# A fifth slot of split weights around three layer boundaries

## What is computed

```python
x = layer_norm(ALPHA * x + h, ln_g[i], ln_b[i])       # h = (o * silu(gate)) @ w_o
x = x + (p[i] @ w_ple[i]) * jax.nn.sigmoid(x @ w_ple_gate[i])
# next block
h = _rmsnorm(x, pre_mix_g) * (1.0 + scale_a) + shift_a
proj = h @ w_in                                        # its first columns: the stage c_f
```

## Time and profile before

| | |
|---|---|
| median of three runs | 2229.97 us (2229.56 to 2232.17) |
| profiled execution, its time | 2231.24 us |
| its span, first to last instruction | 2229.4 us |
| PE busy | 2181.2 us (98%) |
| DVE busy | 1442.8 us (65%) |
| ACT busy | 1011.1 us (45%) |
| mean granted PE clock | 0.995 |

### The profile page before, as it was taken

How to read it: one execution, slowest core, us unless ns; L and a number is a source line. 1 busy time by engine, 2 the same in 40 slices (tenths; PEclk the granted TensorE clock), 3 DMA queues, 4 the chain that set the end, 5 groups by cost and what they waited for, 6 DMA issues and landing times.

```text
span 2229.4 us, 24586 instructions
## 1 busy us (share of the span) xinstructions
PE 2181.2 (98%) x10387; PEld 1811.5 (81%) x10387; DVE 1442.8 (65%) x1420; ACT 1011.1 (45%) x996; POOL 6.5 (0%) x17
## 2 busy tenths in 40 slices
PE   8999999999999999999999999989999999999998
PEld 8878888777888788777888988867888888888887
DVE  5778667775755777767966775487545544544656
ACT  5443563433436633434454566544434434443442
POOL 0000000000000000000000000000000000000000
PEclk9999999999999999999999999999999999999999
DMA  8867649475966466758853325365556656655753
GB/s 287 309 242 270 240 151 388 179 287 193 371 255 238 170 246 268 277 211 329 338 179 104 122 93 196 118 236 213 203 190 231 224 186 215 244 185 199 266 179 125
DMA packets 73310, 499.36 MB, mean 224 GB/s; under 512 B 8945, under 2 KB 9457, under 8 KB 16369
## 3 DMA queue, kind: packets, MB, share of 16 engines
q1 hardware_dynamic: 72784, 497.66, 61.5%
q10 hardware_dynamic: 416, 0.13, 0.0%
HBM read 493.52 MB, written 4.24 MB: 223 GB/s over the span
## 4 chain that ended last, share of the span: by engine, by line
PE 93%; DVE 5%; ACT 2%; issue 1%; DMA 0%; ACTq 0%; DVEq 0%; SPq 0%
PE products L2336 68%; PE products L2347 14%; PE aside L2653 1%; PE transposed L2772 1%; PE transposed L2410 1%; DVE w_low L1422 1%; ACT w_high L839 1%; PE transposed L2500 1%; PE aside L2500 1%; PE transposed L2468 1%; DVE x_low L1538 0%; PE products L2759 0%; PE aside L2759 0%; PE aside L2940 0%; PE transposed L2930 0%
## 5 line engine op out<-in xcount | busy, mean ns | idle before, releaser
L1422 DVE TENSOR_TENSOR w_low<-raw,w_high 128x2048 fp32r<-128x2048 f32 (+3 forms) x336 | 744.2, 2218 | 566.1 <-ACT w_high L839 565.0
L839 ACT ACTIVATE w_high<-raw 128x2048 fp32r<-128x2048 f32 (+3 forms) x336 | 622.4, 1855 | 821.2 <-PE products L2336 668.3
L2336 PE MATMUL products<-w_high,x_high 128*128 128x512 f32 (+2 forms) x1688 | 651.2, 386 | 12.3 <-DVE w_low L1422 9.7
L2336 PE MATMUL products<-w_high,x_low 128*128 128x512 f32 (+2 forms) x1688 | 644.0, 382 | 0.0
L2336 PE MATMUL products<-w_low,x_high 128*128 128x512 f32 (+2 forms) x1688 | 643.6, 381 | 0.0
L2336 PEld LDWEIGHTS products<-w_high,x_high 128*128 128x128 f32 x1688 | 318.2, 189 | 73.3 <-issue 14.2
L2336 PEld LDWEIGHTS products<-w_high,x_low 128*128 128x128 f32 x1688 | 318.2, 188 | 60.1
L2336 PEld LDWEIGHTS products<-w_low,x_high 128*128 128x128 f32 x1688 | 318.4, 189 | 59.4 <-issue 1.4
L1436 DVE SCALAR_TENSOR_TENSOR raw<-raw,cond_row 128x2048 f32<-128x2048 f32 x96 | 220.2, 2294 | 0.4 <-DMA raw<-in_w_mod 0.3
L2347 PE MATMUL products<-w_high,x_high 128*128 128x512 f32 (+1 forms) x472 | 192.7, 408 | 11.4 <-DVE w_low L1422 5.9
L2336 PE MATMUL products<-w_high,u_high 128*128 128x512 f32 x496 | 193.7, 391 | 0.0
(11 more groups left out here) (439 smaller groups left out, 1898.6 us busy)
## 6 DMA issues: line engine op xcount, KB each, us to landing
raw<-in_w_mlp SPq DMA_DIRECT2D x128, 1024.0 KB, 4.9
raw<-in_w_mod SPq DMA_DIRECT2D x96, 1024.0 KB, 5.2
raw<-in_w_ple SPq DMA_DIRECT2D x32, 1024.0 KB, 7.0
raw<-in_w_a_qkv SPq DMA_DIRECT2D x24, 1024.0 KB, 6.2
raw<-in_w_b_kvq SPq DMA_DIRECT2D x24, 1024.0 KB, 7.3
raw<-in_w_a_gate SPq DMA_DIRECT2D x16, 1024.0 KB, 5.7
raw<-in_w_a_out SPq DMA_DIRECT2D x16, 1024.0 KB, 7.1
raw<-in_w_b_gate SPq DMA_DIRECT2D x16, 1024.0 KB, 5.7
```

The source lines that it names most:

```text
L839: act.activation(split_tile(m, 0, st, u, j, 0, n), m.raw[:, RAW_SLOT[at], 0:n], ACT.Copy).then_inc(m.s_w_high, 1)
L1422: dve.tensor_tensor(lo, m.raw[:, RAW_SLOT[at], 0:n], hi.bitcast(F32), ALU.subtract).then_inc(m.s_raw_used, 1)
L2336: ins = pe.matmul(bank, x[:, x0 + kk, a], w, start=first and kk == 0 and n == 0, stop=last and kk == st.kq - 1 and n == 2)
```

## The change

Two more pieces of the arena become slots: `SPARE_SLOTS` 0 is the old extra slot, 1 serves `a_out` and `b_out` (from the fourth quarter on) and the first unit of `ple0` and `ple1`, 2 serves `c_f` from its second quarter to the end of its second unit. With it, quarter 1 of the next stage's first unit is split before row block 0's norm, on ACT and DVE, and `rows_in` is reordered on both. Transpose 3 moves from the last k-tile of half 2 to its second. Since slot 2 lies on the buffer of `h_spans`, that table is loaded after `c_f`'s last unit, into the place of slot 0.

```diff
+SPARE_SLOTS = ((18432, 20480), (13312, 15360), (8192, 6144))
+def slots_for(name, u, j):
+    out = name in ("a_out", "b_out") and (u, j) >= (0, 3)
+    spare = (out or name in ("ple0", "b_kvq", "ple1") or (name == "c_f" and u < 2),
+             out or (name in ("ple0", "ple1") and u == 0),
+             name == "c_f" and (0, 1) <= (u, j) < (2, 0))
+    return [k for k in range(RING)] + [RING + n for n, free in enumerate(spare) if free]
...
-TURNS_AHEAD = {0: (2, 2), 2: (3, 3), 3: (2, 4), 4: (2, 5), 5: (2, 6), 6: (2, 7)}
+TURNS_AHEAD = {0: (2, 2), 2: (1, 3), 3: (2, 4), 4: (2, 5), 5: (2, 6), 6: (2, 7)}
...
@@ sync_program @@
     def c_rows():
         sp.wait_ge(m.s_y_ready, 20)
+        sp.wait_ge(m.s_w_used, 4 * PLAN["ple1"].g0 + 8)
...
-    sp.wait_ge(m.s_ple_full, 8)
-    for dr in range(2):
-        bring(m.h_md_in[dr][:], ...)
     sp.wait_ge(m.s_x4_ready, 4)
...
+            if name == "c_f" and u == 3:
+                sp.wait_ge(m.s_w_used, 4 * (PLAN["c_f"].g0 + 2) + 4)
+                for dr in range(2):
+                    bring(m.h_md_in[dr][:], ...)
@@ pool_program @@
     pool.wait_ge(m.s_h_md_landed, 32)
-    pool.wait_ge(m.s_w_used, 4 * (PLAN["c_f"].g0 + 2) + 4)
@@ scalar_program @@
-        gemm(name_out, nothing, late=3)
+        gemm(name_out, nothing, late=2)
...
             if (layer, 2 * i + k) == (1, 3):
+                act.wait_ge(m.s_ple_full, 8)
+                high_unit("c_f", 0, [1])
                 act.wait_ge(m.s_first_rows, 3)
...
         std(0, 1)
-        high_unit(name, 0, [1])
+        high_unit(name, 0, [2])
         row_high(ROWS_THREE, [0, 1])
-        high_unit(name, 0, [2])
         if between:
             between()
         row_high(ROWS_THREE, [2])
@@ vector_program, rows_in @@
         whole(0)
         normalise(0, 1)
-        low_unit(following, 0, [1])
+        normalise(0, 2)
+        low_unit(following, 0, [2])
         row_low(ROWS_THREE, 0)
-        normalise(0, 2)
         row_low(ROWS_THREE, 1)
-        low_unit(following, 0, [2])
+        whole(1)
         row_low(ROWS_THREE, 2)
-        whole(1)
         normalise(1, 1)
         row_low(ROWS_THREE, 3)
         normalise(1, 2)
+        low_unit(following, 0, [3])
         row_low(ROWS_THREE, 4)
         normalise(0, 3)
         row_low(ROWS_THREE, 5)
-        low_unit(following, 0, [3])
         normalise(1, 3)
...
-        gemm(name_out, add, late=3)
+        gemm(name_out, add, late=2)
...
             if (layer, u) == (1, 3):
+                low_unit("c_f", 0, [1])
                 return
```

More of the change, by code:

```diff
@@ L131 @@
 RAW_SLOT, RAW_COUNT, RAW_BEFORE, RAW_LAST = raw_plan()
[L134 to L141, removed]
+SPARE_SLOTS = ((18432, 20480), (13312, 15360), (8192, 6144))
[5 more added lines that the diff above has]
+    return [k for k in range(RING)] + [RING + n for n, free in enumerate(spare) if free]
 def ring_plan():
-    slots, before, last = [], [], [-1] * (RING + 1)
+    slots, before, last = [], [], [-1] * (RING + len(SPARE_SLOTS))
     for st in PLAN.values():
@@ L150, in ring_plan @@
             for j in range(4):
-                places = range(RING + 1 if has_extra(st.name, u, j) else RING)
-                k = min(places, key=lambda i: last[i])
+                k = min(slots_for(st.name, u, j), key=lambda i: last[i])
                 slots.append(k)
@@ L183, in split_tile @@
     k = slot(st, u, j)
-    if k == EXTRA_SLOT:
-        return (m.hi_extra, m.lo_extra)[which][:, first:last]
+    if k >= RING:
+        return m.spare[k - RING][which][:, first:last]
     return (m.hi, m.lo)[which][:, k, first:last]
@@ L337, in memory @@
     m.hi, m.lo = sb("w_high", [P, RING, 2048], F32R), sb("w_low", [P, RING, 2048], F32R)
-    m.hi_extra, m.lo_extra = at("w_high_extra", 18432, [P, 2048], F32R), at("w_low_extra", 20480, [P, 2048], F32R)
+    m.spare = [[at(f"w_{part}_spare_{n}", word, [P, 2048], F32R) for part, word in zip(("high", "low"), words)] for n, words in enumerate(SPARE_SLOTS)]
     m.xh, m.xl = sb("x_high", [P, KT, T], F32R), sb("x_low", [P, KT, T], F32R)
@@ L439, in memory @@
     m.b_og = at("b_out_gated", 20736, [P, 2, RB, GROUP * HD])
-    m.h_md_in = [at(f"h_spans_in_{dr}", 6144 + 1152 * dr, [P, 9, P]) for dr in range(2)]
+    m.h_md_in = [at(f"h_spans_in_{dr}", 18432 + 1152 * dr, [P, 9, P]) for dr in range(2)]
     m.h_md = at("h_spans", 18432, [P, 2, 9, P], F32R)
@@ L750, in sync_program @@
     gemm("ple1", c_rows)
-    sp.wait_ge(m.s_ple_full, 8)
-    for dr in range(2):
-        bring(m.h_md_in[dr][:], d.spans[:, 9 * P * dr:9 * P * (dr + 1)].rearrange("p (b c) -> p b c", b=9), m.s_h_md_landed)
     sp.wait_ge(m.s_x4_ready, 4)
@@ L765, in unit_by_unit @@
                     bring(m.h_l0[:, dr, slot, :], rows(lb[slot], 1024), m.s_h_rows)
+            if name == "c_f" and u == 3:
+                sp.wait_ge(m.s_w_used, 4 * (PLAN["c_f"].g0 + 2) + 4)
+                for dr in range(2):
+                    bring(m.h_md_in[dr][:], d.spans[:, 9 * P * dr:9 * P * (dr + 1)].rearrange("p (b c) -> p b c", b=9), m.s_h_md_landed)
     for name in ("c_f", "c_hq", "c_hi", "c_mla", "c_hg", "uq", "ukv"):
```

## The result

| | median, us | runs | lowest to highest |
|---|---|---|---|
| before | 2230.05 | 15 | 2229.22 to 2232.17 |
| changed | 2233.95 | 15 | 2231.95 to 2236.82 |

The ratio is 1.0018, 95% interval 1.0010 to 1.0025: 3.9 us slower, between 2.2 and 5.6. The forecast was 2229.8 with a range up to 2232.9. The profiled execution of the changed kernel took 2232.58 us (span 2230.8), 1.4 less than its median; the profiled one of before took 1.2 more than its own.

A forecast was written before the change was run, and what follows sets the result against it. PE holds 93% of the chain, so only its waits and the clock could move, 11.5 us at most. -1.4 (`ple0`, `ple1`), -0.2 (`c_f`) and +1.4 (table) gave -0.2: 2229.8 us, range 2226.8 to 2232.9.

The forecast's parts named there:

- The waits of `ple0` and `ple1`: At these two boundaries PE's waits were to sum to 1.81 against 2.50 us, a gain of 0.7 each, -1.4.
- It just fits: At `ple0` and `ple1`, quarter 1's early split was to end at 405, free if done by 405.13.
- The waits of `c_f`: At the third boundary, waits of 1.04, 1.93, 2.26, 0.51 and 0.57: 6.3 against 4.8 us, +1.5 before the clock.
- I take it that it stays up: -1.7, so -0.2 here.: At `c_f`, the clock was not to fall behind the lone 2.26 wait: -1.7, net -0.2; +1.5 if it falls.
- The table: Moved ahead of `c_hq`'s loads, it was to make later loads land late: +1.4 us, bounds 0 and 2.95.
- the clock falls again: Rival at `c_f`: the clock falls as before, +1.7, 2231.5 us; chance 0.27.
- the clock stays down long: Rival at `c_f`: three close waits keep the clock low, costing 5.1; +4.9 in all, 2234.9 us; chance 0.07.

The follow-up runs named there:

- ple_only: Kernel before with the fifth slot and new row order in `ple0` and `ple1` alone, `c_f` and table as before; ratio 0.9999, median 2230.34 us.
- after_r1: The changed kernel, no edit, profiled once more; 2232.28 us.
- root_first: Changed kernel with row block 1's square root on ACT ahead of the high half of quarter 3; ratio 1.0000, median 2230.42 us.
- cf_old_rows: Changed kernel with the row order of before at `c_f` alone, quarter 1 still taken ahead into the slot; ratio 1.0002, median 2230.69 us.
- best2_again: best2 unchanged, timed again on another chip run; ratio 0.9976, median 2225.74 us of 8 executions.
- best1: Changed kernel with table behind `c_hq`'s loads, root first, and `x_low` 0 and 1 ahead of quarter 2's low half at `c_f`; 0.9992, 2228.39 us.
- best2: best1 with one new order at all three boundaries, row block 1's sums cut from its first normed quarter; ratio 0.9969, median 2224.09 us.
- four_slots: Kernel before, its four slots, table and transposes kept, with best2's row order and the root first; ratio 0.9992, median 2228.81 us.
- late_table: Kernel before with only the spans table loaded after `c_f`'s last unit; ratio 1.0008, median 2232.67 us.
- table_later: Changed kernel with the spans table loaded behind `c_hq`'s last loads and PE's wait just ahead of first use; ratio 1.0013, median 2233.45 us.
- before_again: The kernel before, no edit, profiled again; 2229.82 us.
- cf_only: Kernel before with only the `c_f` boundary and the table changed, `ple0` and `ple1` as before; ratio 1.0019, median 2235.09 us.

## Why the prediction was wrong

**The waits of `ple0` and `ple1`: right in kind, too good in size.** Forecast -0.7 each, measured 30.56 - 30.84 = -0.28. Half 0 waits 0.60 and not 0.41, and the old sum was 0.88 + 0.95 + 0.57 = 2.40 and not 2.50. A term was missing: "It just fits" was put at no cost. Late weights make it not fit at `ple0` in four of eleven executions, 0.4 us on the mean, and in none at `ple1`. What is left is -0.2 for the two together; ple_only's ratio of 0.9999 (0.9990 to 1.0008) agrees.

**The waits of `c_f`: right, one by one.** Forecast waits 1.04, 1.93, 2.26, none, 0.51; measured 1.01, 1.92, 2.38, none, 0.48 (after_r1). Forecast +1.5 before the clock, measured 35.07 - 33.31 = 1.76 without a fall on either side and 36.36 - 34.80 = 1.56 with one on both. The old waits are 4.6 us in the trace and not 4.8, which the prediction's own terms give too (0.32 + 0.53 + 1.38 + 0.87, then 0.94 and 3 x 0.19), so its +1.5 should have been +1.7. root_first and cf_old_rows show the two causes to be those named: the root behind the high half of quarter 3, and the row order.

**The step that failed: "I take it that it stays up: -1.7, so -0.2 here."** I credited the change with the end of a fall that the one profile of before happened to show, on the ground that no single wait had brought the clock down. The runs show otherwise. The clock fell at `c_f` in three of the four profiled executions of the changed kernel, in six of ten with its waits of 1.9 and 2.3, and in two of four with the old boundary. The ground does not hold either: in best2_again a fall follows the very wait of the earlier trace rows. Where the waits were cut (root_first, cf_old_rows, best1, best2 twice, four_slots) it fell at `c_f` in none of six. The timed executions put the size of it at about +1.0 us (0.2 to 1.8) in place of -1.7. And a fall costs 1.3 to 1.5, not 1.7. The rival "the clock falls again" had the direction, but as one fall on both sides; "the clock stays down long" seems to have come true in single executions, 2238 and 2239 us at a clock of 0.993, though no profile caught one.

**The table: right within its bounds.** Forecast +1.4 with bounds 0 and 2.95; measured +1.05 on the mean, with 0 to 3.3 us lost before the `w_low` named in single executions. late_table's median puts it at 2.2, table_later's at 0.5; with their intervals both agree with 1.05. The same wait cost 1.12 in before_again, so part of it is there without the change.

**The sum.** -0.2 + 1.7 + 1.0 + 1.05 = +3.55 us, against 3.9 measured (2.2 to 5.6). With the forecast's own terms and no credit for the clock it would have been -1.4 + 1.5 + 1.4 = +1.5. The term of the clock is an estimate from the timed executions. The profiles alone would give 0.1 to it: their four executions of the changed kernel have a mean of 2233.1, the 15 timed ones a median of 2233.95, and none is like cf_only's 2239.

**The range.** Its upper end took the fall and the dear table together at 2232.9, on a base that already held one fall, so the clock had no cost in it beyond before's. The quarter split with no margin was in neither end.

## What to carry to other kernels

Before crediting a change with a fall of the clock that goes away, look whether the fall is in every execution. One profile shows it or not by chance, and the mean granted clock of the timed executions says more than a few profiles: its average over many shows whether a change makes falls rarer or more frequent. When a step is taken ahead into idle time, its margin against the latest landing counts, not against the one in the profile; when the bound engine waits at several places, walk the order through all queues and ask for each early step what it now stands in front of. Here the order was at fault: with the root first, the sums cut from the scaling and the table later, a kernel with the same slots is 5 to 7 us faster than before where the change was 4 us slower. How much of that is the slot's is open, since the place of transpose 3 was not tried alone.

## What the runs showed of the hardware

The same waits (1.37 and 0.89 us within 2 us) were followed by 3.4 us at half the granted clock in one execution and not in another, and so it was with 1.93 and 2.35, and with a single 1.80 (one of twenty profiles). In no profile was the low stretch at `c_f` longer, but the mean granted clock of timed executions of one kernel went from 0.996 to 0.993, with 2233.16 and 2239.23 us. A load in the busy stretch lands, against the matmuls that need it, up to 3 us later in one execution than in another of the same kernel: 31.96 and 35.15 us for `c_hq`.
